# A hybrid decoder step: queries of two heads made tile by tile, gating operands in PSUM, V products behind the mLSTM chains

## What is computed

```
sh1, sc1, g1, sh2, sc2, g2 = split(silu(c) @ w_ada + b_ada, 6)
h = standardize(x) * (1 + sc1) + sh1
attn, mem, new_state = mixer(split(h @ w_in))     # block-sparse attention, and an mLSTM memory
x = layer_norm(ALPHA * x + g1 * (concat(attn, mem) @ w_out), ln1_g, ln1_b)
h2 = standardize(x) * (1 + sc2) + sh2
qry  = (h2 @ w_query).reshape(R, 8 heads, 2, 128)
half = einsum('rpsd,snd->rpsn', qry, sub_keys)    # 128 keys a side
idx, g = top 16 of the sums of the two sides' top 16
act = gelu(einsum('rd,rpkd->rpk', h2, expert_u[idx]))
f = einsum('rpk,rpkd->rd', g * act, expert_v[idx])
x = layer_norm(ALPHA * x + g2 * f, ln2_g, ln2_b)
```

## Time and profile before

| | |
|---|---|
| profiled execution, its span | 1167.65 us, 1165.9 us |
| three runs | 1160.3, 1161.06, 1166.57 us |
| mean granted TensorE clock | 0.921 of full speed |
| moved by DMA | 412.77 MB, 354 GB/s on average |
| of it on POOL's queue | 278.97 MB, 60.7% of the 16 engines' span |
| busy shares | PE 78%, DVE 65%, POOL 54%, ACT 17% |
| chain that ended last | DMA 33%, POOL 20%, PE 17%, DVE 14% |

### The profile page before, as it was taken

The page is one execution under the profiler, slowest core; times in us unless marked ns, Lnnn a source line. Parts: engine busy times, 40 slices in busy tenths (PEclk is TensorE's granted clock), DMA queues, the critical chain, the costliest instruction groups (busy, mean ns, idle before and its releaser), DMA issues.

```text
span 1165.9 us, 10187 instructions
## 1 busy us (share of the span) xinstructions
PE 904.1 (78%) x2855; PEld 403.4 (35%) x2855; DVE 759.3 (65%) x1645; ACT 192.7 (17%) x571; POOL 624.7 (54%) x605
## 2 busy tenths in 40 slices
PE   3799994487779856598798887777877777777795
PEld 0565641133333345254343432222322222222231
DVE  2277888634517848866666676766786676676635
ACT  0111112271010111111111210210221111021012
POOL 0045567621000004777767677777777777777760
PEclk8899995689769968699999899999999999999998
DMA  9979998779975646999999999999999999999992
GB/s 329 370 263 382 387 394 316 274 278 338 351 277 181 203 172 210 403 410 409 405 409 409 409 409 410 409 409 410 408 411 409 410 409 409 410 409 406 408 368 78
DMA packets 141261, 412.77 MB, mean 354 GB/s; under 512 B 14715, under 2 KB 21632, under 8 KB 138116
## 3 DMA queue, kind: packets, MB, share of 16 engines
q0 software_dynamic: 76608, 278.97, 60.7%
q1 hardware_dynamic: 49492, 109.68, 26.1%
q10 hardware_dynamic: 15106, 23.49, 5.7%
HBM read 405.91 MB, written 6.24 MB: 354 GB/s over the span
## 4 chain that ended last, share of the span: by engine, by line
DMA 33%; POOL 20%; PE 17%; DVE 14%; issue 9%; SPq 6%; ACT 1%; ACTq 0%; DVEq 0%; PEldq 0%; POOLq 0%
POOL ring L533 19%; DMA ring<-in_expert_v,idx 12%; DMA ring<-in_expert_u,idx 10%; PE bank L572 9%; PE bank L575 6%; DMA ring<-in_cache_k 6%; SPq L426 4%; DMA ring<-in_w_ada 3%; DVE ring L1744 3%; SPq L421 2%; DVE ra L1396 1%; PE bank L583 1%; DMA ring<-in_cache_v 1%; DMA ring<-prompt_mods 1%; DVE small L1658 1%
## 5 line engine op out<-in xcount | busy, mean ns | idle before, releaser
L575 PE MATMUL bank<-ring,mix 128*128 128x512 f32 (+1 forms) x1056 | 512.6, 617 | 118.3 <-DMA ring<-in_expert_v,idx 108.4
L1744 DVE CUSTOM_DVE_ANT_0 ring<-ring,bank 128x1024 f32<-128x1024 f32 x256 | 311.0, 1219 | 175.6 <-DMA ring<-in_expert_u,idx 175.1
L575 PEld LDWEIGHTS bank<-ring,mix 128*128 128x128 f32 (+1 forms) x1056 | 183.1, 188 | 435.4 <-DMA ring<-in_expert_v,idx 269.3
L533 POOL DMA_INDIRECT ring<-in_expert_u,idx x264 | 250.1, 947 | 127.9 <-issue 66.8
L533 POOL DMA_INDIRECT ring<-in_expert_v,idx x264 | 250.6, 949 | 90.1 <-issue 62.0
L1292 ACT ACTIVATE mix<-cst,small 128x128 f32<-128x128 f32 (+1 forms) x264 | 92.2, 392 | 254.6 <-PE bank L575 233.2
L490 POOL TENSOR_TENSOR ra<-ra 128x1024 f32<-128x1024 f32 x32 | 75.0, 2345 | 87.4 <-DVE ra L1396 87.4
L478 POOL TENSOR_TENSOR small<-small 128x1 f32<-128x1 f32 (+1 forms) x9 | 6.0, 672 | 173.7 <-DVE small L1661 147.6
L572 PE MATMUL bank<-ht,ring 128*128 128x264 f32 x384 | 93.6, 406 | 3.7 <-DVE w L1386 2.6
L1396 DVE TENSOR_TENSOR ra<-ring,bank 128x2048 f32<-128x2048 f32 x32 | 73.1, 2287 | 34.5 <-PE bank L572 19.7
L572 PE MATMUL bank<-ring,ht 128*128 128x512 f32 (+1 forms) x240 | 82.5, 601 | 2.6 <-ACT ht L1227 1.5
(11 more groups left out here) (314 smaller groups left out, 734.9 us busy)
## 6 DMA issues: line engine op xcount, KB each, us to landing
ring<-in_cache_k SPq DMA_DIRECT2D x128, 256.0 KB, 9.2
ring<-in_cache_v SPq DMA_DIRECT2D x128, 256.0 KB, 4.6
ring<-in_w_ada SPq DMA_DIRECT2D x10, 2048.0 KB, 10.0
ring<-in_w_in ACTq DMA_DIRECT2D x5, 2048.0 KB, 14.8
ring<-in_expert_u,idx POOLq DMA_INDIRECT x264, 13.2
ring<-in_expert_v,idx POOLq DMA_INDIRECT x264, 13.3
ring<-in_w_in SPq DMA_DIRECT2D x2, 2048.0 KB, 20.5
ring<-in_w_ada ACTq DMA_DIRECT2D x2, 2048.0 KB, 10.9
```

The costliest lines, as they stand in the source:

```text
L533: nc.gpsimd.indirect_dma_start(ring_t[:, col(g_in):col(g_in) + DM], None, table, bass.IndirectOffsetOnAxis(tok[:, n * PK + k:n * PK + k + ...
L575: return nc.tensor.matmul(out, lhsT, rhs, start=False, stop=False, skip_group_check=True)
L1744: E.op(v.tensor_tensor_reduce(out=u, in0=u, in1=h2, scale=1.0, scalar=0.0, op0=ALU.mult, op1=ALU.add, accum_out=w[:, k:k + 1]), "u_slot_free")
```

## The change

1. `GV` moves from ring slot 2 to columns 2048 to 5120 of `MOD`. The modulations of all nine rows are stored to DRAM. SP's store and the three broadcasts, and the loads of the first norm's gain and bias, move into the list of V sets (behind sets 19, 23 and 27). Since the broadcast overwrites the sample rows' modulations, these are loaded back behind the second tile's h2, and the third normalisation waits for that (`ln1_in` 96).
2. `values()` at t = 0 is left out and `ada(7)` takes its place; the two calls at the end of chunk 1 are left out too; one is added behind the second transposes, and the sample loop has three for each half instead of two.
3. `values_out(0)` on DVE moves from chunk 1 behind the copies that follow it.
4. `rank`, `am` and `m8` of the gating lie in PSUM.
5. Queries: chunks 0 to 3 are first made for tile 0 alone (128 rows), then `scores(0)` and `scores(1)` with the transposes of h2's other parts around them, then chunks 0 to 3 for the other 136 rows, then chunks 4 to 7. The second block of w_query is asked for with the first; the third comes ahead of the last norm's rows.
6. On ACT the copies follow that order; `best(0)` now stands ahead of the eight later copies. On DVE the clearing of a tile for PE stays behind the normalisations.

The diff, cut:

```diff
-        GV = ring[:, 2, 0:3 * DM]
+        GV = MOD[:, 2 * DM:5 * DM]
...
                 if c in (8, 9):
                     weights(BO + c - 8, w_o, c - 8)
+                if c == 9:
+                    q.wait_ge(sems("ada_out"), 12)
+                    q.dma_start(mods[:, 2 * DM:], MOD[0:NB + 1, 2 * DM:]).then_inc(sems("mods_out"), 16)
+                elif c == 11:
+                    q.wait_ge(sems("mods_out"), 16)
+                    for v, n in enumerate((2, 4, 3)):
+                        load(GV[:, v * DM:(v + 1) * DM], mods[NB:NB + 1, n * DM:(n + 1) * DM].partition_broadcast(P), "ln1_in")
+                elif c == 13:
+                    q.wait_ge(sems("state_T_out"), 1)
+                    load(RA[:, 2 * DM:3 * DM], A["ln1_g"].partition_broadcast(P), "ln1_in")
+                    load(RA[:, 3 * DM:4 * DM], A["ln1_b"].partition_broadcast(P), "ln1_in")
...
-            weights(BQ, w_q, 0)
+            for j in range(2):
+                weights(BQ + j, w_q, j)
+            q.wait_ge(sems("h2_ready"), 2)
+            load(MOD[0:NB, 2 * DM:5 * DM], mods[0:NB, 2 * DM:5 * DM], "ln1_in")
             q.wait_ge(sems("h2_ready"), 3)
-            weights(BQ + 1, w_q, 1)
...
             E.op(tr(bank[4][0:NB, 0:P], rs), "gate_mm")
-            ada(7)
...
-                values()
                 if t:
+                    values()
                     ada(9)
                     values()
+                else:
+                    ada(7)
...
                 E.op(m, "state_mm")
-                values(2)
+                if c == 0:
+                    values(2)
                 E.wait("chunk_done")
...
             mix_T(0, 0)
             values()
             mix_T(1, 0)
+            values()
...
-                    if k % 4 == 3 and vh[0] < 16:
+                    if k % 3 == 1 and vh[0] < 16:
                         values()
...
+            h2_T(0)
+            q.wait_ge(sems("sk_in"), 16)
+            for e in range(2):
+                m = tr(bank[2][:, e * P:(e + 1) * P], SKN[:, e * P:(e + 1) * P])
+            E.op(m, "tail_mm")
+            E.wait("h2T_out")
+            block_in(BQ)
+            for c in range(4):
+                if c >= 2:
+                    q.wait_ge(sems("q_out"), c - 1)
+                queries(c, bank[4 + c % 2], slice(0, P))
+            E.wait("sk_out")
+            q.wait_ge(sems("q_out"), 2)
+            scores(0)
+            q.wait_ge(sems("q_out"), 4)
+            h2_T(1)
+            scores(1)
+            E.wait("h2T_out")
+            h2_T(2)
+            E.wait("h2T_out")
+            for c in range(8):
+                if c == 4:
+                    block_in(BQ + 1)
+                if c >= 4:
+                    q.wait_ge(sems("q_out"), c + 1)
+                queries(c, bank[Q_BANK[c]], slice(P if c < 4 else 0, R))
+                if c % 4 == 3:
+                    used()
+                    q.sem_inc(sems("v_slot_free"), UR // 2)
...
-            rank, am, AM, rm = W[:, 192:256], W[:, 256:320], W[:, 320:448], W[:, 1536:1664]
+            AM, rm = W[:, 320:448], W[:, 1536:1664]
+            rank, am, m8p = (bank[2][0:NB, 64 * i:64 * i + c] for i, c in ((1, 64), (2, 64), (3, 8)))
...
                     sample_norm_state()
-                    q.wait_ge(sems("kv_used"), KQ + 16)
-                    values_out(0, None)
...
+            norm2(0)
+            norm2(1)
+            E.wait("y_mm")
+            q.wait_ge(sems("ln1_in"), 96)
+            norm2(2)
```

More of the change, by code:

```diff
@@ L459, in _ @@
-            for j in range(2):
-                if j:
-                    q.wait_ge(sems("wq_used"), 1)
-                load(WQ_LATE.rearrange("p (k n) -> p k n", k=KT), w_q[:, :, (2 + j) * N:(3 + j) * N], "wq_in")
+            load(RA[:, 2 * DM:3 * DM], mods[NB:NB + 1, 5 * DM:6 * DM].partition_broadcast(P), "ln2_in")
+            q.wait_ge(sems("wq_used"), 1)
+            load(WQ_LATE.rearrange("p (k n) -> p k n", k=KT), w_q[:, :, 3 * N:4 * N], "wq_in")
         @block.gpsimd
@@ L941, in _, with h2_T @@
                 E.op(mm(bank[6 + j][0:NB, :], cst[:, C_SEL:C_SEL + NB], YP[j]), "y_mm")
-            for t in range(3):
+            def h2_T(t):
                 rows = P if t < 2 else NB
@@ L947, in _ @@
                 E.op(m, "tail_mm")
-                E.wait("h2T_out")
-            q.wait_ge(sems("sk_in"), 16)
-            for e in range(2):
-                m = tr(bank[3][:, e * P:(e + 1) * P], SKN[:, e * P:(e + 1) * P])
-            E.op(m, "tail_mm")
             def scores(n):
@@ L961, in scores, with queries @@
                 E.op(m, "scores")
[L963 removed]
+            def queries(c, to, cols):
                 w = ring[:, SLOT[BQ + c // 4], :] if c < 8 else WQ_LATE
[L966 to L972 removed]
                 for k in range(KT):
[L974 removed]
+                    m = mm(to[:, cols], w[:, k * N + (c % 4) * P:k * N + (c % 4 + 1) * P], HTv[:, k, cols],
@@ L978, in queries, with late_queries @@
                     used()
                     q.sem_inc(sems("v_slot_free"), UR // 2)
-                elif c == 11:
+            def late_queries(c):
+                if c % 4 == 0:
+                    q.wait_ge(sems("wq_in"), 16 * (c // 4 - 1))
+                q.wait_ge(sems("q_out"), c + 3)
+                queries(c, bank[Q_BANK[c]], slice(0, R))
+                if c == 11:
                     E.sync()
                     q.sem_inc(sems("wq_used"), 1)
-            for c in range(8):
-                queries(c)
-                if c == 2:
-                    E.wait("sk_out")
-                    q.wait_ge(sems("q_out"), 2)
-                    scores(0)
-                if c == 5:
-                    q.wait_ge(sems("q_out"), 4)
-                    scores(1)
@@ L1028, in _ @@
                     if n + 2 < PH:
[L1029 removed]
+                        q.wait_ge(sems("q_out"), 2 * (n + 5))
                     scores(n + 2)
@@ L1232, in _, with h2T_out @@
                 E.op(a.activation(YP[j], bank[6 + j][:], ACT.Copy), "mixT_out")
-            for t in range(3):
+            def h2T_out(t):
                 r0, rows = t * P, (P if t < 2 else NB)
@@ L1241, in _ @@
                 E.op(m, "h2T_out")
-            E.wait("tail_mm")
-            E.op(a.activation(SKT, bank[3][:, 0:256], ACT.Copy), "sk_out")
             def h2_to_bank(t):
@@ L1262, in query_out @@
                 new = bank[Q_BANK[c]]
-                E.op(a.activation(QT[:, h:h + PH + 2:PH + 1, e, :], new[:, 0:SEQ].rearrange("p (t r) -> p t r", t=2), ACT.Copy))
+                if c < 4:
+                    E.op(a.activation(QT[:, h + PH + 1, e, :], new[:, P:2 * P], ACT.Copy))
+                else:
+                    E.op(a.activation(QT[:, h:h + PH + 2:PH + 1, e, :], new[:, 0:SEQ].rearrange("p (t r) -> p t r", t=2), ACT.Copy))
                 for j in range(2):
                     E.op(a.activation(QT[:, PH, e, 64 * j + h * NB:64 * j + (h + 1) * NB], new[:, SEQ:R], ACT.Copy), "q_out" if j else None)
+            h2T_out(0)
+            E.wait("tail_mm")
+            E.op(a.activation(SKT, bank[2][:, 0:256], ACT.Copy), "sk_out")
+            for c in range(4):
+                E.wait("tail_mm")
+                E.op(a.activation(QT[:, c // 2, c % 2, :], bank[4 + c % 2][:, 0:P], ACT.Copy), "q_out")
+            h2T_out(1)
+            h2_to_bank(0)
+            h2T_out(2)
+            best(0)
             for c in range(8):
                 query_out(c)
-            best(0)
             def sample_h2():
@@ L1613, in _ @@
             step(v.tensor_copy(evT, bank[6][:, 0:32]), "ev_out")
+            q.wait_ge(sems("kv_used"), KQ + 16)
+            values_out(0, None)
             for b in range(NB):
@@ L1642, in _, with norm2 @@
             E.wait("mixT_out", 2)
-            for t in range(3):
-                E.wait("y_mm", 1 if t < 2 else 2)
+            def norm2(t):
+                E.wait("y_mm")
                 rows = P if t < 2 else NB
@@ L1808, in finish @@
                 done[t] = E.last
+            norm2(0)
+            norm2(1)
+            E.wait("y_mm")
+            q.wait_ge(sems("ln1_in"), 96)
+            norm2(2)
+            E.op(v.memset(MIX[0:NB, 2048:2560], 0.0), "zeros_ready")
             for n in range(2):
```

37 lines of the change are left out of this document (8 added, 29 removed).

## The result

The changed kernel took 1148.65 us in the median of four runs (1142.22 to 1152.14), the kernel before 1160.76 us beside it: ratio 0.9856, 95% interval 0.9821 to 0.9891. It is faster, but by some 12 us (the medians) to 17 us (the ratio) where 27 were forecast: the median lies 1.7 us above the range, and the ratio, taken of the 1161.06 us shown before, gives 1144.3, inside it.

What follows compares the result with a forecast made beforehand. Full DMA engines in POOL's 528 expert gathers bound the kernel, their start waiting on DVE's first top-k. 11.8 − 2.7 + 14.9 + 3.2 = 27.2 us off the median 1161.06 gives 1134 us, range 1126 to 1147.

Steps and rivals of the forecast that it cites:

- Tail: DVE before the gathers: waits of 14.9 and 3.2 us ahead of the two top-k go, a 2.7 us read-back wait comes.
- The read-back: Ahead of the third normalisation: DVE waits 2.7 us, issue included, for the sample rows' modulations, counting in full.
- First products of tile 0: PE under the normalisations: four products of 128 columns take 8.7 us, or at most 17.4, ending at 406 or 414.
- From chunk 0's start to the state transposes: PE in the chunks: chunk 1's 14.9 us stall and half a us for values_out go; 15.7 us less.
- From there to the loop: PE from state transposes to sample loop: 14.3 us plus 4.7 for an added V product and bank clearing; loop starts at 329.5.
- the 12 us: DVE in the gating: with operands in PSUM four long instructions shrink to a few tenths, DVE done some 12 us sooner.
- The 3.1 us: PE's gate transpose: only 3.1 of DVE's 12 us pass, since PE's third w_ada block ends at 213.68.
- The loop: PE's sample loop: 37.6 us before, six V products instead of four add 3.7; it ends at 370.7, 9.4 us sooner.
- The V stream just keeps up: V pages in the sample loop: twelve sets at 3.26 us from about 321, the last landing at 368 when PE wants it.
- the rival of the late stream: Sample loop: V sets land too late, six pairs cost 1 us each, gain 21 us, 1140 us; chance 0.17.
- one of my signs of being wrong: Sample loop: the forecast would be wrong if PE waits for V pages there; no size given.
- I take 2 us; the ends are 0 (SP's line unmoved) and 5: Start of chunk 0: 2 us sooner, range 0 to 5, limited by the last w_ada block, issued at about 252.5.

Runs made afterwards that it cites:

- e2: Kernel before with only the tail of the change (tile-by-tile queries, both first top-k behind the normalisations), no read-back; 1148.99 us, ratio 0.9862.
- e1: Changed kernel with the w_ada blocks for ada(10) and ada(11) asked for earlier in SP's list; 1138.25 us, ratio 0.9778 to the kernel before.
- e12: Kernel of e10 with the gating's rank, am and m8 back in SBUF; 1133.15 us, ratio 0.9744 to the kernel before.
- e4: Changed kernel with the gating's rank, am and m8 back in SBUF; 1151.45 us, ratio 0.9879 to the kernel before.
- e6: Changed kernel with the first V product back at t = 0 and ada(7) ahead of its logits, SP's list unchanged; 1137.27 us, ratio 0.9766 to the kernel before.
- e10: Kernel of e5 with PE's waits for ACT's copies put behind the V products between the transposes; 1131.47 us, ratio 0.9707 to the kernel before.
- e5: Kernel of e1 with the sample rows' modulations read back in two parts, g1 earlier; 1133.56 us, ratio 0.9726 to the kernel before.
- e7: Kernel of e1 with two V products back at the end of chunk 1 and four in the sample loop; 1142.39 us, ratio 0.9795 to the kernel before.
- e3: Changed kernel with the third normalisation between the two top-k and best(0) earlier on ACT; 1155.31 us, ratio 0.9917 to the kernel before.
- e8: Changed kernel measured once more, nothing altered; 1151.95 us, ratio 0.9881 to the kernel before.

## Why the prediction was right and wrong

Right were the sign, the place (POOL's first gathers move with DVE's top-k, and the end with them) and most terms. Against the profiled run of before:

- Tail. Forecast 14.9 + 3.2 − 2.7 = 15.4, measured on DVE 14.9 + 3.2 − 3.6 = 14.5. e2 shows the first two alone. At the gathers the 3.2 is worth 2.4: the sum let the ninth follow the first dot, and eight gathers at POOL's pace now take longer. The read-back was taken too cheap by 0.9 us: 3.56 us from issue (409.44) to DVE's start. The Trainium skill ("DMA: Bandwidth & Descriptors", Anatomy of one DMA) had given an estimate of 2.2; its section is on the path of GpSimd, and this load leaves from SP; the rows here and in e1 (396.35 to 399.74, 3.4 us) do not agree with it.
- First products of tile 0: forecast 8.7 us for 128 columns, measured 7.41, and the new waits behind the third normalisation stayed hidden.
- From chunk 0's start to the state transposes: forecast 15.7 us less, measured 14.6 (61.2 before, 317.80 − 271.21 = 46.6 now). From there to the loop: 18.9 and 18.75. The broadcast's 2.34: gone.
- Gating: the 12 us did go on DVE, and PE's third block did hold them up. The 3.1 us belong to the profiled run of before, in which all four instructions were long; with three, DVE is through ahead of PE's third block in e2 and e12 and 0.1 us behind it in e4, so the 3.1 are not shown to be won. The Trainium skill ("SBUF — State Buffer", Who interferes with whom) describes the DVE and GpSimd port lock; 3.04 us with source and target in SBUF and 0.22 in PSUM agree with it, but it prices the engine, not the path. The copy with 3.71 and 0.26 us shows that the place of the operands alone does not fix the time.
- The loop: 41.2 forecast, 43.8 measured. "The V stream just keeps up" was off by 2 us of waits in it: the rival of the late stream, in small, and one of my signs of being wrong. One of the six other issues in the line, the store of the modulations, held SP for 4.51 us where I had allowed 0.8.
- Two sums are off by 0.2 us or less (14.9 + 2.5 + 0.5 is 17.9, not 17.7; 9.4 + 2.34 is 11.7, not 11.8); nothing hangs on them.

The step that failed is "I take 2 us; the ends are 0 (SP's line unmoved) and 5". Measured: 4.1 us later. I had seen that the first product would stand at 239 to 240 and so free the slots after 238.33, and priced only the last w_ada block. The block for `ada(10)` stands in the same line, directly behind sets 4 and 5. Before it left at 243.58, when `ada(8)` had ended and freed its slot, and PE did not wait for it; now `ada(8)` ends at 235 and the block waits in line until 247.53. PE came sooner to a load that left later.

What chunk 0 waits for last, though, is the last block. Its issue did not come forward to 252.5 but stayed (255.19 against 254.89), since the line ahead of it began 4 us later; it landed after 12.46 us, not 9.91; and its product, at a granted clock of 0.58 (1.00 before), took 3.21 us, not 1.90. The landing 2.85 us later and the product 1.3 us longer are the 4.1. The 7.38 us at `ada(10)` do not come on top: had that block been early, PE would have stood at the last one until 267.65 all the same, unless the late block had itself held up the last, which no run separates. And 1.4 of the 4.1 us were there before the gating (K pages' last reduction at 193.06, before at 191.62).

The bound "0" excluded a loss without a reason, and no rival held one at this place; the range reached up to 1147 for the late V stream alone. This step took 6.1 us of the 10.8 that were missing (27.2 forecast, 14.5 + 1.9 measured), the loop 2.6, chunk and read-back 1 each. With the list mended (e1) the ratio is 0.9778, 25.9 us of 1165.4: the sum that was forecast, less 1.3. That is in part luck: chunk 0 begins 8.6 us sooner than before there (258.49 against 267.08), where the forecast has 2, and this covers what the loop, chunk 1 and the read-back lack.

What the list cost in the changed kernel is shown by e1, and from the other side by the 5 us that e6 wins ahead of chunk 0. What stays open: which of the two late blocks counts, whether the gating edit is worth anything in a run with all four instructions long, and what e10 wins over e5 beyond the intervals.

## What to carry to other kernels

Where one engine issues loads in a fixed list and slots come free by another's work, moving that work changes the list's meaning: for each entry behind the moved release, ask when it could leave and when it does. A bound of a moved step has two signs until each queue that it passes has been priced. And a stall that is cleared by moving work is worth only what the place it moves to has idle (11 us gave some 2 in e7), so look first at how full that place is.

## What the hardware showed that I had not expected

- From 317 to 337 us of the changed kernel PE was granted 0.60 of its clock on average (the row below, columns as in the earlier trace rows) and was busy for 14.4 of 20 us; a V product there took 3.51 us, in the loop 1.90. Ahead stood idle times of 4.45, 2.53 and 2.27 us. So a wait on PE cost more than itself: e10 took two waits of 2.5 and 2.3 us away, of the two products behind them the second ran in 1.90, and from the state transposes to the loop it took 12.5 us (303.16 to 315.66) where e5 took 18.9 (307.32 to 326.17).

```profile
317.00:337.00 20.00, 14.41 (x62) 5.99 (x63) 1.81 (x6) 5.10 (x18) 0.00 (x0) 0.60 1.03 377
```

- One store of SP took 4.51 us to issue, with 9 rows by 16 KB, in the midst of V sets (318.57); in e1 2.91, in e3 1.38. In the changed kernel no set waited for it: the next left at 328.41, when the V product of 326.31 had freed its slot. In e6 the next left 1.6 us behind the store's end (307.90 to 309.51).
- On 8 partitions the same instruction took 3.04 or 0.22 us by where its operands lay (e4, e8). But the copy behind it took 3.71 us in the kernel before and 0.26 in e4, both times from SBUF to SBUF, and both times a POOL instruction with two tensors started in the same instant (205.57; 208.39).
